# Retention on halves of the array: heads side by side in rows and columns, both directions' states stacked on partitions, decayed keys, no zero padding

## What is computed

```python
# per head, per direction; qc, kc, vc are chunks of 128 tokens
scores = einsum('cd,sd->cs', qc, kc) * decay_mask
intra  = scores @ vc
kv     = (kc * k_decay).T @ vc            # 64 x 64 per chunk
state  = chunk_decay * state + kv         # scan over the chunks
cross  = (qc * q_decay) @ states_prev
out    = intra + cross                    # forward and backward summed
# then per head: centred, divided by its deviation, times silu(g) * gn_w
```

## Time and profile before

| | us |
|---|---|
| median of 3 runs (3383.41 to 3385.73) | 3383.92 |
| the profiled execution's own time | 3385.56 |
| its span, first to last instruction | 3383.8 |
| PE busy | 3321.8 (98%) |
| DVE, ACT, POOL busy | 2246.2, 1252.0, 1068.4 |

### The profile page before, as it was taken

One profiled execution on the slowest core, in us unless ns is written; L12 is line 12 of the kernel. 1 busy time (PEld: TensorE's weight loads), 2 busy tenths in 40 slices (PEclk: granted clock), 3 DMA queues, 4 the chain that ended last, 5 costly groups with the idle time before them and its releaser, 6 DMA issues. The chain is left out here.

```text
span 3383.8 us, 48755 instructions
## 1 busy us (share of the span) xinstructions
PE 3321.8 (98%) x17988; PEld 2825.5 (84%) x17988; DVE 2246.2 (66%) x3432; ACT 1252.0 (37%) x2128; POOL 1068.4 (32%) x1121
## 2 busy tenths in 40 slices
PE   8999999999999999999999999999999999999998
PEld 4888888888888888888888788889998788888886
DVE  6575567887178888888756543578992656656566
ACT  4332356776241122112223432366772322222222
POOL 0222310111424444444434122410014344343443
PEclk9999999999999999999999999999999999999999
DMA  6445562222112222222110424462212111111111
GB/s 255 151 184 213 148 197 64 54 71 71 40 56 75 74 74 74 74 80 75 54 39 26 180 103 153 145 199 53 58 43 89 38 55 44 50 50 43 50 44 61
DMA packets 100272, 305.34 MB, mean 90 GB/s; under 512 B 12448, under 2 KB 39200, under 8 KB 97824
## 3 DMA queue, kind: packets, MB, share of 16 engines
q1 hardware_dynamic: 100128, 303.40, 27.6%
HBM read 240.17 MB, written 63.18 MB: 90 GB/s over the span
## 5 line engine op out<-in xcount | busy, mean ns | idle before, releaser
L131 POOL TENSOR_TENSOR wlo<-raw,whi 128x256 fp32r<-128x256 f32 x516 | 494.6, 988 | 814.9 <-ACT whi L119 814.9
L2270 DVE SCALAR_TENSOR_TENSOR xT<-down_acc,mod,xT 128x512 f32<-128x512 f32 (+1 forms) x800 | 496.3, 694 | 236.1 <-PE down_acc L194 234.1
L1993 POOL TENSOR_TENSOR hid_lo<-y,hid_hi 128x256 fp32r<-128x256 f32 (+1 forms) x189 | 185.2, 1011 | 622.5 <-ACT hid_hi L2167 622.5
L2156 ACT ACTIVATE up<-up_acc 128x512 f32<-128x512 f32 (+1 forms) x210 | 115.4, 551 | 580.0 <-PE up_acc L194 579.0
L192 PE MATMUL up_acc<-mix_hi,whi 128*128 128x512 f32 (+1 forms) x875 | 323.6, 370 | 1.8 <-DVE mix_lo L487 0.9
L193 PE MATMUL up_acc<-mix_lo,whi 128*128 128x512 f32 (+1 forms) x875 | 322.5, 369 | 0.0
L194 PE MATMUL up_acc<-mix_hi,wlo 128*128 128x512 f32 (+1 forms) x875 | 322.0, 368 | 0.0
L192 PE MATMUL up_acc<-late_hi,whi 128*128 128x512 f32 (+1 forms) x860 | 316.7, 368 | 0.0
L194 PE MATMUL up_acc<-late_hi,wlo 128*128 128x512 f32 (+1 forms) x860 | 316.4, 368 | 0.0
L193 PE MATMUL up_acc<-late_lo,whi 128*128 128x512 f32 (+1 forms) x860 | 316.4, 368 | 0.0
L192 PE MATMUL down_acc<-hid_hi,first_whi 128*128 128x512 f32 (+1 forms) x825 | 304.6, 369 | 1.4 <-DVE xT L2317 1.4
(11 more groups left out here) (329 smaller groups left out, 7501.7 us busy)
## 6 DMA issues: line engine op xcount, KB each, us to landing
raw<-in_w_rest SPq DMA_DIRECT2D x112, 512.0 KB, 3.6
norm_buf<-in_w_ada SPq DMA_DIRECT2D x78, 512.0 KB, 4.5
first_raw<-in_w_rest SPq DMA_DIRECT2D x57, 512.0 KB, 3.6
proj_scratch<-stage SPq DMA_DIRECT2D x18, 640.0 KB, 4.4
raw<-in_w_first SPq DMA_DIRECT2D x21, 512.0 KB, 6.7
ada_raw<-in_w_ada SPq DMA_DIRECT2D x6, 1536.0 KB, 14.5
xT<-proj_scratch SPq DMA_DIRECT2D x4, 1920.0 KB, 8.9
xT<-in_xT SPq DMA_DIRECT2D x8, 640.0 KB, 24.9
```

Source lines behind the costliest of these rows:

```text
L131: m = nc.gpsimd.tensor_tensor(self.lo[k][:, x:x + 256], self.raw[k][:, x:x + 256], self.hi[k][:, x:x + 256].bitcast(f32), ALU.subtract)
L1993: m = nc.gpsimd.tensor_tensor(hid_lo[:, x:z], y[1][:, x:z], hid_hi[:, x:z].bitcast(f32), ALU.subtract)
L2156: nc.scalar.activation(up[half][:, pc:pc + w], ub[c][:, :w], ACT.Copy).then_inc(up_evac, 1)
L2270: nc.vector.scalar_tensor_tensor(xs, db[g % DB][:, :w], mod_of(layer, 5, m, c), xs, ALU.mult, ALU.add).then_inc(added, 1)
```

## The change

`retention` is rewritten; the rest of the program stays, but for two arguments in the attention block and the layout of two small tables.

- `kz`, `vz`, `qz`, `bd` and all zero fills are gone. The values are kept as `v` (one ACT copy, 384 columns). DVE multiplies the keys, straight from their bank, by the decays of both directions into `kd` (one instruction of 768 columns). The key-value product of a head has `kd` as weights, 128 wide (64 of each direction), and `v` of 64 columns as the moving side. Its result has forward states on partitions 0 to 63 and backward states on 64 to 127; a scan step works on 64 partitions and 384 columns.
- The queries are loaded twice, into partitions 0 to 63 and 64 to 127 of `q2`, in groups of chunks by 6 DMAs each; the turned keys and values alternate between two banks each.
- POOL forms all of `qd` first, one instruction of 768 columns per chunk, as soon as `decq` (now ready after chunk 3) and the group of queries are there, without waiting for `fwd_done`. After the last of them it takes over the gate product (`gated`) from DVE.
- `inner` is 6 products of 128 columns, each on 64 rows of the array. `outer` is 12 products of 128 columns with weights 64 wide, and `variance` 2 products of 384 columns with weights 64 wide, each on half of the array's columns.
- On PE `outer(i - 1)` now stands ahead of `variance(i - 2)`.

```diff
@@ attention: PE and ACT
-                ret.variance(pe, ret.turns - 2)
+                ret.variance(pe, ret.turns - 2, True)
                 ret.outer(pe, ret.turns - 1)
                 transposes(0)
-                ret.variance(pe, ret.turns - 1)
+                ret.variance(pe, ret.turns - 1, True)
...
+                act.wait_ge(ret.qd_done, ret.qd_count)
                 exp(0)
@@ retention: SP and POOL
+                def load_queries(g):
+                    x0, x1 = groups[g][-1] * P, (groups[g][0] + 1) * P
+                    for rows in halves:
+                        for t in range(3):
+                            sp.dma_start(q2[rows, 2 * t:2 * t + 2, x0:x1], proj[T_RQ + t, :, x0:x1].rearrange("(h d) n -> d h n", d=HD)).then_inc(q2_in[g], 16)
...
+            def gated(pool, i):
+                pool.wait_ge(gate_in[i % 2], 16 * (i // 2 + 1))
+                pool.wait_ge(root_done, i + 1)
+                if i >= 2:
+                    pool.wait_ge(out_done, i - 1)
+                nc.gpsimd.tensor_tensor(on[:, i % 2, :], rt[:, i % 2, :], gate[:, i % 2, :, :].rearrange("p t n -> p (t n)"),
+                                        ALU.mult).then_inc(on_done, 1)
...
-                pool.wait_ge(decq_made, 6)
-                pool.wait_ge(fwd_done, 1)
+                pool.wait_ge(decq_made, RH)
                 for i, c in enumerate(order):
-                    pool.wait_ge(rq_in[group_of(i)], 16)
-                    if i >= 2:
-                        pool.wait_ge(main_done, i - 1)
-                    for d in range(2):
-                        nc.gpsimd.tensor_tensor(qd[:, i % 2, d, :, :], queries(i), decq[:, d, :, :], ALU.mult).then_inc(qd_done, 1)
+                    pool.wait_ge(q2_in[group_of(i)], 96)
+                    nc.gpsimd.tensor_tensor(qd[:, :, columns(c)], q2[:, :, columns(c)], decq[:, :, :], ALU.mult).then_inc(qd_done, 1)
+                for i in range(NO):
+                    gated(pool, i)
@@ retention: PE
                 for t in range(3):
-                    dst = po[i % 2][:, t * P:(t + 1) * P]
+                    dst = [po[i % 2][rows, t * P:(t + 1) * P] for rows in halves]
                     for half in range(2):
                         h = 2 * t + half
-                        nc.tensor.matmul(dst, vz[:, c, t, half * P:(half + 1) * P], at[:, i % 2, h * P:(h + 1) * P],
-                                         start=(half == 0), stop=False)
-                    for d in range(2):
-                        mm = nc.tensor.matmul(dst, bd[:, i % 2, t, d, :], qd[:, i % 2, d, t, :], start=False, stop=(d == 1))
+                        nc.tensor.matmul(dst[half], v[:, c, h * HD:(h + 1) * HD], at[:, i % 2, half, t, :], start=True, stop=False)
+                    for half in range(2):
+                        h = 2 * t + half
+                        mm = nc.tensor.matmul(dst[half], state[:, c, h, :], qd[:, h, columns(c)], start=False, stop=True)
...
-                nc.tensor.matmul(pk[:, :3 * P], og, osq[:, i % 2, :], start=True, stop=True).then_inc(var_done, 1)
+                for rows in ([slice(0, P)] if whole else halves):
+                    mm = nc.tensor.matmul(pk[rows, :3 * P], og[:, rows], osq[:, i % 2, :], start=True, stop=True)
+                mm.then_inc(var_done, 1)
...
+                    for h in range(RH):
+                        mm = nc.tensor.matmul(pa[c % 2][:, h * HD:(h + 1) * HD], kd[:, c % 2, h, :, :].rearrange("p d e -> p (d e)"),
+                                              v[:, c, h * HD:(h + 1) * HD], start=True, stop=True)
...
                 for i in range(NO):
                     inner(i)
+                    if i == 1:
+                        pe.wait_ge(fwd_done, 1)
+                    if i:
+                        outer(pe, i - 1)
                     if i >= 2:
                         variance(pe, i - 2)
-                    if i:
-                        outer(pe, i - 1)
@@ retention: DVE
+                def decayed_keys(c):
+                    dve.wait_ge(k_turned, c + 1)
                     if c >= 2:
                         dve.wait_ge(kv_done, c - 1)
+                    nc.vector.tensor_tensor(kd[:, c % 2, :, :, :],
+                                            turned_k[c % 2][:, :W].rearrange("p (h e) -> p h e", e=HD).unsqueeze(2).to_broadcast([P, RH, 2, HD]),
+                                            dec.unsqueeze(3).to_broadcast([P, RH, 2, HD]), ALU.mult).then_inc(kd_done, 1)
                 def scan(new, old, d):
-                    x = state[:, new, :, d, :]
-                    st.link(dve, nc.vector.tensor_tensor(x, state[:, old, :, d, :], cdec[:, :, d:d + 1].to_broadcast([P, 3, HD]), ALU.mult))
+                    x = state[halves[d], new, :, :]
+                    st.link(dve, nc.vector.tensor_tensor(x, state[halves[d], old, :, :], cdec[halves[d], :, :].to_broadcast([HD, RH, HD]), ALU.mult))
                     dve.wait_ge(kv_kept, old + 1)
-                    st.link(dve, nc.vector.tensor_tensor(x, x, kv[:, old, :, d, :], ALU.add))
+                    st.link(dve, nc.vector.tensor_tensor(x, x, kv[halves[d], old, :, :], ALU.add))
```

More of the change, by code:

```diff
@@ L518, in ret_views @@
         n, small = 3 * TOK, {}
-        for name, shape in (("mask", (RH, P)), ("qpos", (2, P)), ("pos", (RH, 2)), ("lg", (RH, 2)), ("lgp", (3, 2)), ("cdec", (3, 2)),
+        for name, shape in (("mask", (RH, P)), ("qpos", (1, P)), ("pos", (RH, 2)), ("lg", (RH, 2)), ("lgp", (RH, 1)), ("cdec", (RH, 1)),
                             ("centre", (1, P)), ("mean", (1, P))):
@@ L1456, in retention, with columns @@
             halves = [slice(0, HD), slice(HD, P)]
-            groups = [(rq_first, order[0:2]), (rq_more[0], order[2:6]), (rq_more[1], order[6:10])]
+            groups = [order[0:4], order[4:8]] if last else [order[0:2], order[2:6], order[6:10]]
             def group_of(i):
-                return 0 if i < 2 else 1 if i < 6 else 2
-            def queries(i):
-                dst, cs_ = groups[group_of(i)]
-                at_ = (order[i] - cs_[-1]) * P
-                return dst[:, :, at_:at_ + P]
-            def own_columns(x, half):
-                return x[:, :, half * (P + HD):half * (P + HD) + HD]
-            def half_of(bank, half):
-                return bank[:, :W].rearrange("p (t h e) -> p t h e", h=2, e=HD)[:, :, half, :]
+                return next(g for g, cs_ in enumerate(groups) if order[i] in cs_)
+            def columns(c):
+                return slice(c * P, (c + 1) * P)
             def store(sp, i):
@@ L1496, in load_gate @@
                     sp.dma_start(gate[:, i % 2, :, :], proj[T_RG:T_RG + 3, :, c * P:(c + 1) * P].rearrange("t p n -> p t n")).then_inc(gate_in[i % 2], 16)
-                load_queries(0)
                 gates_stored(sp)
+                for g in range(len(groups)):
+                    load_queries(g)
                 load_gate(0)
@@ L1646, in _ @@
                         keep(c - 1)
[L1647 to L1648 removed]
+                    for h in range(2 * (c - 1), 2 * c) if 1 <= c < 4 else []:
+                        nc.scalar.activation(decq[:, h, :], qpos[:, 0, :], ACT.Exp, scale=lgp[:, h, :]).then_inc(decq_made, 1)
                 keep(BLK - 1)
[L1652 to L1664 removed]
                 for i in range(NO + 1):
@@ L1733, in _ @@
                         finish(dve, i - 2)
-            return Retained(NO, head_in, main_done, var_done, logged, out_done, out_stored, store, variance, log, root, finish, outer, square)
+            return Retained(NO, head_in, main_done, var_done, logged, out_done, out_stored, store, variance, log, root, finish, outer, square,
+                            qd_done, NO)
     def output_projection(layer, last, seg, hi, lo, unit, block, att):
```

155 lines of the change are left out of this document (42 added, 113 removed).

## The result

The changed kernel takes **3427.34 us**, median of 4 runs (3416.54 to 3432.47), beside 3383.66 us of the kernel before in the same comparison (4 runs, 3383.28 to 3385.73). The ratio is 1.0124, with an interval of 1.0098 to 1.0149: slower by 1.2%, 43.7 us. The forecast was 3403 us with a range to 3425: the direction was right, the size was less than half, and the time lies above the range. The profiled execution took 3429.3 us with a span of 3427.4, 43.6 more than the span before. The kernel before had medians of 3383.2 to 3385.1 beside the later experiments, so numbers may be compared across them.

A forecast was written before the change was run, and what follows sets the result against it. PE, busy 98% of the span, was taken as the bound. First part with collision +11.5, turns +6.9 and clock +1 gave +19.4 us, 3403 us by medians; the forecast's own range was 3392 to 3415, with rivals 3378 to 3425.

The forecast's parts named there:

- What bounds the kernel: Whole kernel: PE is busy 98% of the span, so only what shortens or lengthens PE's own stream counts.
- the mechanism of the collision: First part: POOL lets one dependent DVE scan instruction through per query product, 1.95 us each with handover; both layers +11.5 us.
- 6.5 us later than before ... 5.0 later: First outer product in layer 0 and layer 1, delayed by POOL's query products colliding with DVE's scan; sum +11.5 us.
- So PE and DVE come out level: First part without collisions: PE reaches the first outer product at 411.6, DVE ends the mask at 411.4; 3.2 us earlier.
- 5.56 us against 4.62: Length of one turn after and before, as outer, variance and the gate's chain run one behind the other; sum +6.9 us.
- Clock. ... I take +1, bounds -3.5 and +5: PE's new waits may drop the first part to 1.2 GHz; the dip at 459.5 may stay or go; +1 us.
- From scores to transposes nothing changes: Start of the attention block: scores, variance, logarithm, root, exponential take 5.2 us before and after.
- The halves do not overlap: Rival on PE's turns: outer 2.69 and variance 1.28, turn 7.2 us; +22, 3425 us; chance 0.14.
- No collision: Rival on the first part: the slow scan instructions were chance, or half-height ones pass; 3384 us, no change; chance 0.15.
- cheap small products: Rival: no collision, and key-value products cost half as weight loads overlap; faster, 3374 us; chance 0.11.

The follow-up runs named there:

- run with writes: Changed kernel with POOL's query products replaced by six zero fills of 128 columns each, so POOL writes the same tile and reads nothing: 3401.86 us (one run).
- run with late products: Changed kernel with POOL's query products waiting for the end of the forward scan, then one per turn with gate products between: 3404.64 us (one run).

## Why the prediction failed in size

**What bounds the kernel, and the mechanism of the collision: right.** POOL's first query product was forecast at 395.2 and came at 396.01, the scan took about 2 us per instruction until the tenth product ended, and one dependent instruction passed per product. The run with writes and the run with late products show it from two sides. The Trainium skill (SBUF — State Buffer, Who interferes with whom) says that two SBUF inputs contend with a GpSimd instruction that reads and not with one that only writes; 2.04 us beside reads, 0.55 beside writes agree.

**"6.5 us later than before ... 5.0 later": too small.** It came out 17.5 and 9.0, of which 5.0 and 1.3 are the clock (below); at full clock it is 12.6 and 7.7, 8.7 more than forecast in sum.
- Without the collision the part gains 1.5 and 2.2 us, not 3.2 twice.
- The collision cost DVE's scan instructions 14.4 us in layer 0 (26.4 less 12.0) and 9.9 in layer 1, where the forecast had 9.9 (10.9 less 1 for the pauses) and 8.2. I had put ten scan instructions and three large ones into POOL's ten products. There were ten and two, each scan instruction held for a product of 2.0 us, and the pauses, where I had expected them, met the large ones and gave nothing back.

**"So PE and DVE come out level": right at 2.4 GHz alone.** PE issues in order. While it waits at a key-value product for `kd`, the transposes of the next chunk stand behind that wait. At 419.47 PE still had one product, a chunk's transposes, two products and two inner products to do. At full clock these are some 6.6 us (1.3, 1.0, 2.6 and 1.7), which DVE's own rest hides; at 1.2 GHz they took 12.5, and PE set the end of the part.

**"5.56 us against 4.62": the mechanism right, the price too high.** At full clock the turn is 5.22 to 5.28: the outer products took 1.33 and the variance 0.77, for 1.39 and 0.96, and the inner products 0.87 for 1.34. The variance's 0.77 is less than the three records of 0.32 that I had taken in a row, so its halves run nearly side by side from the start. The moved variance is what makes the turn long: with it ahead again it is 3.5. At full clock the term would have been about +2 (1.7 and 0.4), not +6.9.

**"Clock. ... I take +1, bounds -3.5 and +5": this is the step that failed.** I named the drop and put its place in the first part alone, "beside a DVE that sets the pace", where it would be hidden. It was not hidden, since PE's tail had to run at that clock, and it went on: in layer 0's turns PE is busy 70% and the granted clock is 0.73, each turn 6.9 us for 5.2. The clock costs 5.0 and 1.3 us in the first parts, 12.1 and 2.7 in the turns and 2.0 at the output projection, and gives back 3.5 behind the first transposes: some +19.6 in place of +1. These are estimates, from the rows of the same work at full clock. The sum was 24.2 short of the span's 43.6. The clock is 18.6 of that, the first part 8.7 and the way from scores to transposes 2.4; the turns, 4.8 too high, and 0.6 of starts go the other way. So at full clock the forecast would have come out some 6 us short, and in part by luck, as two of its terms were off in opposite directions. The text had the right number in a half sentence: a clock held at 1.2 GHz in the turns would give about 3425. It stood beside another mechanism, without a chance or a place of its own, and the range ended there.

**"From scores to transposes nothing changes": wrong, +1.2 twice.** The `tout` of the last turn but two now waits for POOL's gate product, behind the variance that came just before the scores, and stands ahead of the maxima of the scores on DVE. The probabilities wait for these and the transposes for the probabilities:

```profile
487.92 0.56 DVE L1626 TENSOR_TENSOR tout<-po,gated 128x384 f32<-128x384 f32 x1 [5.43 <-POOL gated L1495]
488.40 0.68 DVE L1340 TENSOR_REDUCE part_max<-scores 128x1 f32<-128x512 f32 x1
489.00 0.95 DVE L1348 TENSOR_REDUCE part_max<-scores 128x1 f32<-128x768 f32 x1
```
```profile
490.30 1.33 ACT L1300 ACTIVATE probs<-scores,negmax 128x1280 f32<-128x1280 f32 x1 [1.04 <-DVE negmax L1351]
```

With the variance ahead it is 5.2 again.

**The rivals.** *The halves do not overlap* is excluded: 1.33 us alternating against 2.21 in blocks, and the lower clock gave this rival's 3425 by another way. The Trainium skill (TensorEngine Tiling (Array Packing), Theoretical Speedup) gives up to 2x for a dimension of 64; 24 records of 0.055 against 0.112 in the earlier trace rows agree. *No collision* and *cheap small products* are excluded by the rows: key-value products with 64 moving columns take 12 records in 1.29 us, as the earlier trace rows had it.

## What to carry over

When a change makes PE wait, price its work behind the wait at both clocks, and ask for how long the lower one will last; make that a case with a chance, not an allowance. For a stretch in which another engine sets the pace, look at what PE still has to do in order behind its last wait: here it was hidden at 2.4 GHz and 5 us too long at 1.2 GHz. And when halving an engine's work in a software pipeline, look first whether the order that fed the next stage is kept: here one call in another place cost 37 of 44 us, with the clock that PE's waits brought down.

## What the runs showed that I had not expected

- Work that computes nothing seems to have made the kernel faster: with two products of 512 columns per turn (1.98 us at full clock) PE stayed at 2.4 GHz, and layer 0's turns took 9.9 us less than in the changed kernel's profile (11.7 off the total). It is one run, and layer 0's turns without filling took 43.8 to 53.4 us in the executions with this order of work and POOL's gate product.
- The same instructions with the same waits run at either level: turns of 5.22 and 6.9 us, PE tails of 4.4 and 8.0 us (key-value and inner products, 2225.71 to 2230.52 less its wait, and 2194.44 to 2202.45). That goes with the spread of the changed kernel's runs, 16 us against 2.5 of the kernel before: its four times, 3416.5, 3425.4, 3429.3 and 3432.5 us, have mean clocks of 0.990, 0.988, 0.987 and 0.985. A single run of such a kernel can't be compared within 5 us. What exactly lets the clock rise again stays open; I did not try it.
- A collision has no fixed price either. The same ten products beside the same scan let DVE start its ninth `kd` anywhere from 31.0 to 35.4 us behind the first transposes, by whether a scan instruction or a `kd` falls into POOL's pauses.
- Products on two halves gain by their order: 0.055 us per record when they alternate, 0.11 inside a block of one half, as at full width.
